# Last projection of the token mixer: token rows stationary, 512 weight columns moving

## What is computed

```
h = x @ w_in                                  # (320, 2048) @ (2048, 4352)
y = concat(conv branch, chunk-MLP branch, pooling branch)     # (320, 2048)
x = layer_norm(ALPHA * x + y @ w_out)         # w_out (2048, 2048): the last projection
x = layer_norm(ALPHA * x + hier_moe(x))       # router, then 16 experts, top 2 of 4 in one group
```

## Time and profile before

| what | value |
|---|---|
| median of 3 runs | 897.81 us (897.41 to 899.27) |
| profiled execution, its own time | 895.74 us |
| span of the profiled execution | 894.0 us |
| TensorE busy | 837.3 us (94%) |
| input projection ends, last projection's first matmul | 273.38 us |
| last projection's last matmul, router's first transpose | 390.79 us, 394.83 us |
| mean DMA rate | 300 GB/s |

### The profile page before, as it was taken

One profiled execution on the slowest core, in us unless ns is written; L12 is line 12 of the kernel. 1 busy time (PEld: TensorE's weight loads), 2 busy tenths in 40 slices (PEclk: granted clock), 3 DMA queues, 4 the chain that ended last, 5 costly groups with the idle time before them and its releaser, 6 DMA issues.

```text
span 894.0 us, 11220 instructions
## 1 busy us (share of the span) xinstructions
PE 837.3 (94%) x4741; PEld 557.4 (62%) x4741; DVE 282.2 (32%) x388; ACT 263.3 (29%) x462; POOL 24.9 (3%) x41
## 2 busy tenths in 40 slices
PE   6999999999999999994999999998999989997993
PEld 6989999999999999984433333432333333333331
DVE  5383375335664444445000102043000330022203
ACT  5243332323223232321522332432223232222101
POOL 0000000000001000001000000000000000000000
PEclk9999999999999999995999999999999999999997
DMA  9644653654444884379898999999999999999980
GB/s 293 192 141 124 204 177 118 210 190 141 141 149 150 290 292 139 121 261 406 334 426 320 424 421 426 426 419 422 424 424 422 423 425 423 420 424 425 422 358 36
DMA packets 81148, 267.80 MB, mean 300 GB/s; under 512 B 5625, under 2 KB 58319, under 8 KB 59656
## 3 DMA queue, kind: packets, MB, share of 16 engines
q1 hardware_dynamic: 78042, 258.92, 74.7%
q0 software_dynamic: 1984, 5.31, 1.5%
q10 hardware_dynamic: 1078, 2.94, 1.0%
HBM read 263.07 MB, written 11.54 MB: 307 GB/s over the span
## 4 chain that ended last, share of the span: by engine, by line
PE 72%; DMA 15%; DVE 4%; ACT 4%; issue 2%; SPq 2%; POOL 0%; POOLq 0%; ACTq 0%; DVEq 0%
PE ps L1270 17%; PE ps L475 12%; PE ps L476 12%; PE ps L477 12%; PE ps L1304 9%; DMA down_w<-in_expert_w_down 4%; DMA gu_w<-in_expert_w_up 4%; DMA xg<-z_rows,row 4%; PE ps L1206 3%; DMA out<-xg,sample_row 3%; SPq L397 1%; ACT xT L1376 1%; DMA raw<-in_w_in 1%; DVE xg L1623 1%; PE ps L1247 1%
## 5 line engine op out<-in xcount | busy, mean ns | idle before, releaser
L1270 PE MATMUL ps<-gu_w,xT 128*64 128x512 f32 x1024 | 234.8, 600 | 7.7 <-DMA gu_w<-in_expert_w_up 6.7
L656 DVE TENSOR_TENSOR w_lo<-raw,w_hi 128x2048 fp32r<-128x2048 f32 x50 | 114.6, 2291 | 170.6 <-ACT w_hi L648 169.1
L475 PE MATMUL ps<-xT_hi,w_hi 128*128 128x320 f32 x512 | 159.2, 311 | 0.0
L477 PE MATMUL ps<-xT_hi,w_lo 128*128 128x320 f32 x512 | 158.2, 309 | 0.0
L476 PE MATMUL ps<-xT_lo,w_hi 128*128 128x320 f32 x512 | 158.2, 309 | 0.0
L1270 PEld LDWEIGHTS ps<-gu_w,xT 128*64 128x64 f32 x1024 | 71.5, 138 | 135.6 <-issue 131.2
L648 ACT ACTIVATE w_hi<-raw 128x2048 fp32r<-128x2048 f32 x49 | 93.8, 1915 | 207.9 <-DMA raw<-in_w_in 136.1
L1376 ACT ACTIVATE xT<-ps,gbT 128x64 f32<-128x64 f32 x256 | 82.4, 407 | 156.8 <-PE ps L1206 156.8
L1304 PE MATMUL ps<-down_w,aT 128*64 128x512 f32 x480 | 107.7, 601 | 4.5 <-ACT aT L1384 4.0
L475 PEld LDWEIGHTS ps<-xT_hi,w_hi 128*128 128x128 f32 x512 | 96.1, 188 | 0.5
L476 PEld LDWEIGHTS ps<-xT_lo,w_hi 128*128 128x128 f32 x512 | 96.1, 188 | 0.0
(11 more groups left out here) (257 smaller groups left out, 517.6 us busy)
## 6 DMA issues: line engine op xcount, KB each, us to landing
gu_w<-in_expert_w_gate SPq DMA_DIRECT2D x64, 1024.0 KB, 12.8
gu_w<-in_expert_w_up SPq DMA_DIRECT2D x64, 1024.0 KB, 15.0
down_w<-in_expert_w_down SPq DMA_DIRECT2D x32, 2048.0 KB, 19.6
raw<-in_w_in SPq DMA_DIRECT2D x34, 1024.0 KB, 5.3
raw<-in_w_out SPq DMA_DIRECT2D x16, 1024.0 KB, 5.3
tok<-in_x_prompt SPq DMA_DIRECT2D x2, 1024.0 KB, 6.4
z_rows<-tok ACTq DMA_DIRECT2D x2, 768.0 KB, 4.1
tok<-in_x_sample SPq DMA_DIRECT2D x1, 512.0 KB, 9.6
```

The costliest lines, as they stand in the source:

```text
L475: pe.matmul(out, wh[:, t, col], hi[:, kt, :], start=(n == 0 and t == 0), stop=False)
L477: last = pe.matmul(out, wl[:, t, col], hi[:, kt, :], start=False, stop=(n == 1 and t == CK - 1))
L656: dve.tensor_tensor(w_lo[k][:, :], raw[k][:, :], w_hi[k][:, :].bitcast(FP32), ALU.subtract)\
L1270: last = pe.matmul(ps[C * side:C * (side + 1), GU, :], x, w[:, :, c, FH * side:FH * (side + 1)], start=(j == 0 and c == 0), stop=(j == PAI ...
```

## The change

The last projection is turned round. 128 tokens of y are stationary, 512 columns of w_out move, and the result is tokens x channels. The output has four quarters of 512 columns (`QO`), each of four chunks of 4 k-tiles x 512 columns (`TO`, `CO_W`); there are still 16 chunks of 1 MB. For a k-tile and a quarter there are three matmuls for each of the two prompt tiles, and two for the 64 sample tokens: their high and low parts lie side by side in `yT` and make one stationary operand of 128 columns, so that w_hi gives both the high and the low product (in the upper and lower 64 partitions) and w_lo its product (and, in the upper 64 partitions, a low x low product that the three-product form leaves out). `yT` holds both parts of a channel in one row of 640, with a table `PLACE` for where a k-tile lies; `y_lo` writes it in two instructions where it was one. The copies to `mixT`, the transposes back and `out_tokens` are gone. DVE adds the residual straight from the PSUM banks, in one instruction for each prompt tile and two for the samples. Each quarter has three banks of its own (`ROW_BANKS`), and bank 6 and 7 are among them.

```diff
-    mixT = [at(f"mixT{s}", LATE + s * 2 * ROW, [P, 2, NTOK]) for s in range(3)]
...
+    QUARTERS = (2, 3, 0, 1)
+    TO = 4
+    CO_W = CH // TO
+    QO = D // CO_W
+    ROW_BANKS = ((4, 5, 6), (0, 1, 7), (2, 3, 6), (4, 5, 7))
...
+            kq, col = QUARTERS[o % 4], CO_W * (o // 4)
+            sp.dma_start(raw[c % 3][:, :].rearrange("p (t n) -> p t n", t=TO),
+                         wout_v[:, TO * kq:TO * kq + TO, col:col + CO_W]).then_inc(raw_full[c % 3], 16)
...
-        pe.wait_ge(ylo_ready, 4)
-        group_products(pe, G_O, Y, HALF_O, wait_half=(ylo_ready, 7))
-        with pe.Fori(0, 2) as s:
-            for i in range(3):
-                group_products(pe, G_O + 1 + i, Y, HALF_O, s, 3)
-                out_tokens(i, s)
-        group_products(pe, G_END - 1, Y, HALF_O)
-        out_tokens(6)
-        out_tokens(7)
...
+        wait_read(pe, "z0", "z1")
+        for q in range(QO):
+            out_rows(pe, q)
+
+    def out_rows(pe, q):
+
+        if q == 0:
+            wait_group_read(pe, G_B)
+        elif q == 1:
+            wait_group_read(pe, G_B + 1)
+        elif q == 2:
+            wait_group_read(pe, G_B + 2)
+        if q >= 2:
+            pe.wait_ge(rows_summed, 3 * (q - 1))
+        for n, kq in enumerate(QUARTERS):
+            c = 2 * G_O + 4 * q + n
+            if q == 0:
+                pe.wait_ge(ylo_ready, 4 if n < 2 else 7)
+            pe.wait_ge(lo_ready, c + 1)
+            wh = w_hi[c % 3][:, :].rearrange("p (t n) -> p t n", t=TO)
+            wl = w_lo[c % 3][:, :].rearrange("p (t n) -> p t n", t=TO)
             for i in range(2):
+                out, rows = ps[:, ROW_BANKS[q][i], :], slice(P * i, P * (i + 1))
+                for t in range(TO):
+                    y = yT[:, PLACE[TO * kq + t], :]
+                    lo = slice(LO_P + P * i, LO_P + P * (i + 1))
+                    pe.matmul(out, y[:, rows], wh[:, t, :], start=(n == 0 and t == 0), stop=False)
+                    pe.matmul(out, y[:, lo], wh[:, t, :], start=False, stop=False)
+                    last = pe.matmul(out, y[:, rows], wl[:, t, :], start=False, stop=(n == 3 and t == TO - 1))
+                if n == 3:
+                    last.then_inc(rows_made, 1)
+            for t in range(TO):
+                out, both_parts = ps[:, ROW_BANKS[q][2], :], yT[:, PLACE[TO * kq + t], SEQ:LO_P]
+                pe.matmul(out, both_parts, wh[:, t, :], start=(n == 0 and t == 0), stop=False)
+                last = pe.matmul(out, both_parts, wl[:, t, :], start=False, stop=(n == 3 and t == TO - 1))
+            last.then_inc(w_used, 1)
...
+        for c in range(2 * G_O + 2, CHUNKS1 - 1):
+            split_hi(act, c)
+        store_z(act, 3, slice(0, 3 * CO_W))
+        split_hi(act, CHUNKS1 - 1)
...
-            dve.tensor_tensor(yT_lo[:, first:first + n, :], tmp[:, 0:n, :],
-                              yT_hi[:, first:first + n, :].bitcast(FP32), ALU.subtract)\
-               .then_inc(ylo_ready, 1)
+                two = two_of(first + k)
+                steps.inc(dve.tensor_tensor(yT[:, two, LO_P:2 * NTOK], tmp[:, k:k + 2, 0:SEQ],
+                                            yT[:, two, 0:SEQ].bitcast(FP32), ALU.subtract))
+                last = dve.tensor_tensor(yT[:, two, LO_S:LO_P], tmp[:, k:k + 2, SEQ:NTOK],
+                                         yT[:, two, SEQ:NTOK].bitcast(FP32), ALU.subtract)
...
+        def residual(q):
+
+            col = slice(CO_W * q, CO_W * (q + 1))
+            for i in range(2):
+                dve.wait_ge(rows_made, 2 * q + i + 1)
+                dve.scalar_tensor_tensor(out=tok[:, i, col], in0=tok[:, i, col], scalar=ALPHA,
+                                         in1=ps[:, ROW_BANKS[q][i], :], op0=ALU.mult, op1=ALU.add)\
+                   .then_inc(rows_summed, 1)
+                dve.wait_ge(rows_summed, 3 * q + i + 1)
+                steps.inc(dve.bn_stats(xstats[:, i, q, :], tok[:, i, col]))
+            dve.wait_ge(w_used, 2 * G_O + 4 * (q + 1))
+            bank = ROW_BANKS[q][2]
+            link(dve.scalar_tensor_tensor(out=tok[0:64, 2, col], in0=tok[0:64, 2, col], scalar=ALPHA,
+                                          in1=ps[0:64, bank, :], op0=ALU.mult, op1=ALU.add))
+            dve.tensor_tensor(tok[0:64, 2, col], tok[0:64, 2, col], ps[64:128, bank, :], ALU.add)\
+               .then_inc(rows_summed, 1)
+            dve.wait_ge(rows_summed, 3 * q + 3)
+            steps.inc(dve.bn_stats(xstats[0:64, 2, q, :], tok[0:64, 2, col]))
+
+        for c in range(2 * G_O + 4, CHUNKS1):
+            split_lo(dve, c)
+            if (c - 2 * G_O) % 4 == 1:
+                residual((c - 2 * G_O) // 4 - 1)
 
...
-        for n in (USE_O + 2 * 7, USE_O + 2 * 7 + 1):
-            b, full = tb(n)
-            pe.wait_ge(tb_free[b], full)
+        pe.wait_ge(rows_summed, 3 * QO)
```

More of the change, by code:

```diff
@@ L122, in hybrid_trunk_kernel @@
     xT_lo = at("xT_lo", XA + XT_B, [P, KT, NTOK], F32R)
[L123 to L124 removed]
+    yT = at("yT", YT_HI0, [P, KT, 2 * NTOK], F32R)
+    PLACE = (0, 1, 2, 8, 9, 10, 3, 4, 5, 11, 12, 13, 6, 7, 14, 15)
+    LO_S, LO_P = NTOK, 2 * NTOK - SEQ
     ROW = NTOK * 4
@@ L339, in hybrid_trunk_kernel, with two_of @@
     x_tiles = [x_prompt[0, 0:P, :], x_prompt[0, P:SEQ, :], x_sample.rearrange("b t d -> (b t) d")]
-    HALF_O = (1, 0)
+    QUARTERS = (2, 3, 0, 1)
[3 more added lines that the diff above has]
+    ROW_BANKS = ((4, 5, 6), (0, 1, 7), (2, 3, 6), (4, 5, 7))
+    def two_of(first):
+        a, b = PLACE[first], PLACE[first + 1]
+        return slice(a, b + 1, b - a)
     def wait_alone(eng, sem, value, turns):
@@ L454, in pool_program, with group_products @@
                            channel_multiplier=1).then_inc(pool_const, 1)
-    def group_products(pe, g, acts, halves, turn=0, turns_at=0, wait_half=None, between=None):
+    def group_products(pe, g, acts, halves, turn=0, turns_at=0, between=None):
         hi, lo = acts
@@ L611, in pe_mixer @@
             last.then_inc(tb_full[b], 1)
[L613 to L621, removed]
-            for i in range(2):
[L623 to L630, removed]
@@ L659, in store_z @@
     def store_z(eng, k, cols):
-        for n in (USE_O + 2 * (k - 1), USE_O + 2 * (k - 1) + 1):
-            b, full = tb(n)
-            eng.wait_ge(tb_free[b], full)
+        eng.wait_ge(rows_summed, 3 * k)
         for i, (t0, m) in enumerate(TILES):
@@ L679, in y_hi @@
         def y_hi(first, n):
-            act.activation(yT_hi[:, first:first + n, :], tmp[:, 0:n, :], ACT.Copy).then_inc(yhi_ready, 1)
+            for k in range(0, n, 2):
+                last = act.activation(yT[:, two_of(first + k), 0:NTOK], tmp[:, k:k + 2, :], ACT.Copy)
+            last.then_inc(yhi_ready, 1)
         for i, (t0, m) in enumerate(TILES):
@@ L784, in act_mixer @@
                 act.dma_start(rbias[:, NG:NG + NE], re_b[0:1, :]).then_inc(rw_in, 16)
[L786 to L794, removed]
-        with act.Fori(0, 2) as s:
-            for i in range(3):
-                split_hi(act, 2 * (G_O + 1 + i), s, 6)
-                split_hi(act, 2 * (G_O + 1 + i) + 1, s, 6)
-                copy_out_group(i, s)
-        split_hi(act, 2 * G_END - 2)
-        split_hi(act, 2 * G_END - 1)
-        copy_out_group(6)
-        store_z(act, 6, slice(0, 6 * GW))
-        copy_out_group(7)
+        for c in range(2 * G_O + 2, CHUNKS1 - 1):
+            split_hi(act, c)
+        store_z(act, 3, slice(0, 3 * CO_W))
+        split_hi(act, CHUNKS1 - 1)
     def dve_mixer(dve):
@@ L815, in y_lo @@
             dve.wait_ge(yhi_ready, count)
-            dve.tensor_tensor(yT_lo[:, first:first + n, :], tmp[:, 0:n, :],
-                              yT_hi[:, first:first + n, :].bitcast(FP32), ALU.subtract)\
-               .then_inc(ylo_ready, 1)
+            for k in range(0, n, 2):
+                two = two_of(first + k)
[3 more added lines that the diff above has]
+                                         yT[:, two, SEQ:NTOK].bitcast(FP32), ALU.subtract)
+                if k < n - 2:
+                    steps.inc(last)
+            last.then_inc(ylo_ready, 1)
             dve.wait_ge(ylo_ready, count)
@@ L998, in dve_mixer @@
-        with dve.Fori(0, 2) as s:
-            steps.enter(s, 9)
-            for i in range(3):
-                split_lo(dve, 2 * (G_O + 2 + i), s, 6)
-                split_lo(dve, 2 * (G_O + 2 + i) + 1, s, 6)
-                residual(i, s)
-        steps.leave(2)
+        def residual(q):
[15 more added lines that the diff above has]
+            steps.inc(dve.bn_stats(xstats[0:64, 2, q, :], tok[0:64, 2, col]))
```

37 lines of the change are left out of this document (5 added, 32 removed).

## The result

The changed kernel takes 904.64 us (median of 6 runs, 903.66 to 905.86), the kernel before in the same runs 898.76 us (897.41 to 900.75): a ratio of 1.0069, with a 95% interval from 1.0053 to 1.0084, about 6 us slower. The forecast was 903.8 us, from 900.5 to 908.1. The profiled execution of the changed kernel took 904.99 us, with a span of 903.1 us.

The account below looks back on a forecast made before the run. TensorE was taken as the bound, a router shift moving the end equally. Start +7.9, products -1.6, clock +1.7 and tail -2.0 sum to +6.0 us: 901.7 us for the profiled execution, 903.8 us against the median, range 900.5 to 908.1.

Parts of the forecast that it names:

- The bound, and how a shift reaches the end: TensorE's chain sets the experts' weight stream's start, so a shift of the router moves the end equally.
- The products: Last projection: 512 matmuls of 512 columns at 0.2267 us, 115.8 against 117.4 us from first to last start: -1.6 us.
- Rival 1: The matmul's fixed 0.0134 us is hidden at 512 columns: 898.3 us, no difference to be seen; chance 0.08.
- The start: Last projection's first product waits for ACT's reads z0 and z1, starting at 281.3 instead of 273.38 us: +7.9 us.
- The clock: After the idle gap at the last projection's start, TensorE runs at 1.2 GHz: +1.7 us, bounds 0 and 3.4.
- The tail: From the last projection's last product to the router's first transpose, 2.0 us instead of 4.04: -2.0 us.
- The sum: At the router, 7.9 - 1.6 + 1.7 - 2.0 = +6.0 us, moving the end by the same amount.
- Rival 3: 512-column matmuls cost 0.235 us, or the clock falls again before the router: 905.5 to 908.1 us; chance 0.17.
- Rival 2: The wait for z0 and z1 does not hold TensorE at the last projection's start: 894.2 us; chance 0.05.
- the cover: Last projection's last w_out chunk is ready 5 us before its first product, so a 4 us later DMA costs nothing.

Follow-up runs that it names:

- Experiment 4: The kernel before, with only the wait for z0 and z1 added ahead of its last projection: 907.08 us, ratio 1.0091 to the kernel before.
- experiment 1: The changed kernel with ACT's copies z0 and z1 moved ahead of the last groups' two y_hi: 894.48 us, ratio 0.9953 to the kernel before.
- experiment 9: The changed kernel with each w_out chunk loaded by two transfers in 1 KB pieces, not one in 2 KB pieces: 903.65 us, ratio 1.0060.
- 5: The changed kernel with 28 unused 512-column products on TensorE ahead of the wait for z0 and z1: 901.47 us, ratio 1.0040.
- 6: Experiment 3's kernel with the samples in three products of 64 stationary columns instead of two of 128: 907.77 us, ratio 1.0102.
- 7: Experiment 3's kernel with nearly every product cut into two of 256 columns: 900.75 us, ratio 1.0035.
- 10: Experiment 1's kernel with the samples' products and sums ahead of the prompt tiles in the last chunk: 895.95 us, ratio 0.9975.
- 2: The changed kernel with the wait for z0 and z1 moved from the stage's start to the first sample product: 896.13 us, ratio 0.9972.
- 8: Experiment 3's kernel with the samples' products and sums ahead of the prompt tiles in the last chunk: 895.74 us, ratio 0.9968.
- 3: The changed kernel with copies z0 and z1 ahead of the y_hi and their wait at the first sample product: 895.82 us, ratio 0.9973.

## Why the prediction was right

**The bound, and how a shift reaches the end: right.** From the router's first transpose to the end of the span it is 499.2 us before and 500.0 us in the changed kernel, and between 499.0 and 502.1 us in all the kernels above, though the router starts anywhere from 391.7 to 406.5 us. A shift at the router is a shift at the end. Experiment 4 shows it by time.

**The products: right.** (401.19 - 396.66) / 20 = 0.2265 us where 0.2267 was forecast from the 320-column matmuls; over the whole stage of experiment 1 it is 115.94 / 511 = 0.2269. Both lie between the bounds that I took from the 512-column rows, 0.225 and 0.235. Rival 1 is refuted. The Trainium skill's gap of N / 2.4 + 2.5 ns ("TensorE: Matmul & The Clock Gate", "Back-to-back issue gap") does not hold for these matmuls at any of three widths: the trace has N / 2.4 + 13.2 to 13.7 ns.

What the forecast does not say is that this gain does not come from the products. 511 distances of 0.2269 us are 115.9 us, 767 of 0.1467 were 112.5: the new products take 3.4 us more, since the samples' added columns cost 6.8 us (16,384 at 2.4 GHz) and 256 fixed parts fewer give back only 3.4. The stage is shorter all the same, 115.9 against 117.4 us, because it has no six sets of transposes inside (0.57 us each, 3.4 in all), no stop for `y_lo` (0.65 us in the trace before, at 281.32 us), and no longer distance behind the first product of each group (0.24 us for 0.15).

**The start: the mechanism right, the term too large.** Forecast +7.9 us, measured +6.66. The chain from ACT's split of chunk 35 to the end of the reads is as long as I worked it out: 282.99 - 273.86 = 9.13 us. But this split starts 1.90 us ahead of the z transposes, and not 0.64 us as in the kernel before (272.17 against 272.81). I had written that nothing ahead of the reads gets shorter; the wait for chunk 35 did, from 6.06 to 5.04 us. It is so in each profile with the changed loading order of w_out (5.04 to 5.29 us), and not in experiment 4 (5.90 us), which has the old one. The size of the pieces is not the reason (experiment 9); whether it is which rows of w_out a chunk takes was not tried and stays open.

**The clock: right in kind, too small.** Forecast 1.7 us, from falls of 3.4 us behind gaps of 1.8 and 2.7 us. Behind this gap of 6.4 us the clock stayed at 1.2 GHz until about 287.6 us, 4.6 us into the products. From the first product to the last it took 118.20 us, and 115.94 and 115.92 us in experiments 1 and 5, where the clock holds: it cost 2.3 us, inside the bounds 0 and 3.4.

**The tail: right.** -2.15 us against -2.0. The old tail held twelve transposes, of two groups, and not the six that I named; as its 4.04 us were measured whole, the sum does not change by it.

**The sum.** 6.66 + 0.79 - 2.15 = +5.3 us at the router against 6.0; the 1.2 us too much in the start were partly made up by the 0.6 too little in the clock. The medians differ by 5.9 us. That this is so near to 6.0 is in part luck: two errors of opposite sign, and 0.85 us behind the router that I had not forecast. Rival 3's second fall of the clock in the pause ahead of the router did not happen in the changed kernel. Rival 2 did not happen either, but experiment 1 brings it about: 894.48 us, where the rival's price was 894.2. Against the kernel before that is -4.2 us by the runs and -2.6 by the trace, where the price was -3.6.

**What the cover held.** No product of the stage waited for weights: the idle time of all its groups but the first is 0.0.

## What to carry to other kernels

When a stage is moved to other buffers, ask for each buffer who reads it last, and where that reader stands in its own engine's order: the copies that nobody waited for became the head of the critical path. Put the wait at the first instruction that needs it, or the late reader in front; each was one or two lines here and took 7.6 to 7.9 us off the way to the router, more than the rewrite of the stage, which takes off 3.6 us where nothing waits. Ask also where a rewrite's gain comes from: here the wide products themselves take 3.4 us more, and the gain is the transposes that they make needless, inside the stage and behind it. And count a TensorE wait of some us with what the clock takes behind it, about a third more here.

## What the runs showed of the hardware

The cost of an fp32r matmul in a row of them, each with its own weight load, is its columns at 2.4 GHz plus 0.0137, 0.0134 and 0.0132 us at 256, 320 and 512 columns (0.0136 at 512 over a whole stage); with 64 instead of 128 stationary columns, 0.230 us at 512, no less.

What I had not expected: the scatter between runs of one kernel goes in good part with the clock in the first 22 us. The kernel before took 895.4 to 901.0 us beside the first four experiments, its four fastest runs each with a mean granted clock of 0.979, its four slowest of 0.970 to 0.973. The twelve profiles fall into three groups by the clock from 14 to 22 us. At 1.00 the z transposes start at 272.4 to 273.0 us (the kernel before; experiments 5, 6, 7 and 10), at 0.79 at 273.9 to 274.4 us (1, 2, 8 and 9), and at 0.57 at 275.8 to 275.9 us (the changed kernel; 3 and 4). TensorE does 45 to 48, 35 to 38 or 27 matmuls in that stretch. Which group an execution falls into does not follow its edits. Two profiled executions should be compared from a point behind that, or 3 us of chance are taken for the change.
